# Index tiles first, logits between the matmul steps of later tiles, and a shorter keep in the threshold search

## The reference, cut to what matters

```
u = rmsnorm(h, norm_mix[0])
a_q, a_ckv, i_q, i_k, i_w, b_qkv, b_z, b_beta, b_a = split(u @ w_in)
# indexer, for each block of 128 query rows (4 heads of 64)
logits = einsum('bqhd,bsd->bqhs', q_idx, k_idx)
score  = einsum('bqh,bqhs->bqs', w, relu(logits))      # causal by chunks of 64
idx    = top_k(score, 256)                             # which latents a query sees
...
y_b = gated_deltanet(b_qkv, b_z, b_beta, b_a, ...)     # starts with silu(causal_conv(b_qkv))
```

## Time and profile before

| | |
|---|---|
| median of 3 timed runs | 2788.07 us (2785.03 to 2789.04) |
| the profiled execution | 2780.74 us, its span 2778.9 us |
| PE busy, share of the span | 94% |
| DVE busy | 60% |
| ACT, POOL busy | 35%, 10% |
| mean granted TensorE clock | 0.957 |

### The profile page before, as it was taken

How to read it: one execution, slowest core, us unless ns; L and a number is a source line. 1 busy time by engine, 2 the same in 40 slices (tenths; PEclk the granted TensorE clock), 3 DMA queues, 4 the chain that set the end, 5 groups by cost and what they waited for, 6 DMA issues and landing times.

```text
span 2778.9 us, 32118 instructions
## 1 busy us (share of the span) xinstructions
PE 2625.5 (94%) x12096; PEld 2086.8 (75%) x12096; DVE 1661.8 (60%) x2672; ACT 969.3 (35%) x1615; POOL 264.5 (10%) x268
## 2 busy tenths in 40 slices
PE   8998987888998899999999999898899999999998
PEld 7666666878755477888888878676687888888787
DVE  4179997677455357756664354763768665653444
ACT  4232221111154344333333233443744333332333
POOL 3004525444000000000001000000000000000000
PEclk7989998899699999999999999999999999999999
DMA  5211110000100043232235434111132322335443
GB/s 161 69 38 31 38 31 1 0 0 1 46 1 1 23 136 114 84 91 84 68 92 194 162 125 139 36 46 46 31 99 106 91 70 82 91 95 215 145 137 106
DMA packets 207166, 217.27 MB, mean 78 GB/s; under 512 B 12496, under 2 KB 174304, under 8 KB 203568
## 3 DMA queue, kind: packets, MB, share of 16 engines
q1 hardware_dynamic: 204080, 196.13, 22.6%
q0 software_dynamic: 2944, 19.24, 1.9%
HBM read 172.35 MB, written 42.47 MB: 77 GB/s over the span
## 4 chain that ended last, share of the span: by engine, by line
PE 79%; DVE 14%; issue 3%; ACT 2%; POOL 0%; DMA 0%; DVEq 0%; SPq 0%; POOLq 0%; ACTq 0%
PE ps L329 21%; PE ps L330 20%; PE ps L331 20%; DVE met L1948 4%; PE ps L2673 2%; DVE bT L1925 2%; PE ps L2155 1%; PE ps L2168 1%; PE ps L2650 1%; DVE thr L1978 1%; PE ps L2661 1%; PE ps L2164 1%; PE ps L1757 1%; PE ps L423 1%; PE ps L1056 1%
## 5 line engine op out<-in xcount | busy, mean ns | idle before, releaser
L318 DVE TENSOR_TENSOR wlo<-wraw,whi 128x1024 fp32r<-128x1024 f32 x152 | 186.7, 1230 | 389.9 <-ACT whi L312 389.6
L312 ACT ACTIVATE whi<-wraw 128x1024 fp32r<-128x1024 f32 x166 | 174.8, 1054 | 354.4 <-PE ps L331 341.3
L329 PE MATMUL ps<-ahi,whi 128*128 128x512 f32 x704 | 276.5, 393 | 6.2 <-DVE hT L956 3.8
L330 PE MATMUL ps<-alo,whi 128*128 128x512 f32 x704 | 275.1, 391 | 0.0
L331 PE MATMUL ps<-ahi,wlo 128*128 128x512 f32 x704 | 275.1, 391 | 0.0
L329 PE MATMUL ps<-uhi,whi 128*128 128x512 f32 x608 | 245.3, 403 | 19.8 <-DVE bT L1935 10.1
L329 PE MATMUL ps<-q_T,whi 128*128 128x512 f32 x640 | 249.2, 389 | 1.6 <-ACT upr L757 1.6
L331 PE MATMUL ps<-q_T,wlo 128*128 128x512 f32 x640 | 249.0, 389 | 0.0
L330 PE MATMUL ps<-q_T,whi 128*128 128x512 f32 x640 | 249.0, 389 | 0.0
L329 PE MATMUL ps<-q_B,whi 128*128 128x512 f32 x608 | 238.9, 393 | 2.4 <-DVE q_B L488 2.4
L330 PE MATMUL ps<-ulo,whi 128*128 128x512 f32 x608 | 239.7, 394 | 0.0
(11 more groups left out here) (464 smaller groups left out, 4894.5 us busy)
## 6 DMA issues: line engine op xcount, KB each, us to landing
wraw<-in_ffn_w_down_dram SPq DMA_DIRECT2D x88, 512.0 KB, 3.5
wraw<-in_ffn_w_gate_dram SPq DMA_DIRECT2D x44, 512.0 KB, 5.3
araw<-acts SPq DMA_DIRECT2D x88, 256.0 KB, 3.7
wraw<-in_ab_w_in_dram SPq DMA_DIRECT2D x24, 512.0 KB, 3.8
park<-hT POOLq DMA_DIRECT2D x3, 4096.0 KB, 11.4
wraw<-in_ffn_w_up_dram SPq DMA_DIRECT2D x24, 512.0 KB, 5.3
acts<-sgA SPq DMA_DIRECT2D x12, 1024.0 KB, 4.6
raw<-in_ffn_w_up_dram SPq DMA_DIRECT2D x20, 512.0 KB, 4.0
```

Source lines behind the costliest of these rows:

```text
L312: nc.scalar.activation(as_raw(whi[:, t.slot, :]), raw, ACT.Copy).then_inc(S("w_high"), 1)
L318: eng.tensor_tensor(as_raw(wlo[:, t.slot, :]), raw, as_raw(whi[:, t.slot, :]).bitcast(F32), ALU.subtract).then_inc(S("w_split"), 1)
L329: nc.tensor.matmul(dst, wh, xh, start=start, stop=False, **kw)
L330: nc.tensor.matmul(dst, wh, xl, start=False, stop=False, **kw)
```

## The change

1. The tiles come in the order index queries, index queries, index key, compressed KV. The doubling (`twice`) moves from tile 3 to tile 2, and the copy of the compressed KV to DRAM by POOL waits for the fourth move, not the first.
2. The small product follows tile 2. Its transposes follow the first 8 steps of tile 3.
3. The logits go in 12 pairs of heads (parities 0 and 1 alternate for each piece of 512), each followed by 2 steps of the tiles 3, 4 and 5. A pair waits until both relus of the pair before are done. The other steps of tiles 5 and 6 follow. ACT and DVE do units 0 to 7 in iteration 3 and 8 to 23 in iteration 4, where DVE also masks, computes the gates and calls `select_start`.
4. `bits_of` gives one step to each of tiles 5, 6 and 7, then 14 to tiles 8 to 19 (two at 11 and 19), then 1, 2, 1, 2: again 23.
5. `select_keep` with a bit known when the program is built shifts the flag to the bit's place and ors it in, one instruction in place of two, and raises `sel_ok` by an instruction of its own. The 8 steps of the delta rule's loop keep the old form.

```diff
-    order = [("ab", CKV0), ("ab", IQ0), ("ab", IQ0 + P), ("ik", IK0)]
+    order = [("ab", IQ0), ("ab", IQ0 + P), ("ik", IK0), ("ab", CKV0)]
     order += [("ab", AQ0 + P * j) for j in range(4)]
...
     for i in range(2):
-        w_load(sp_, Tile(n_ab + i), ab_v[:, :, (CKV0, IQ0)[i]:(CKV0, IQ0)[i] + P])
+        w_load(sp_, Tile(n_ab + i), ab_v[:, :, IQ0 + i * P:IQ0 + (i + 1) * P])
     for i in range(1, 5):
...
-n_ab = first.get(("ab", CKV0), 0)
+n_ab = first.get(("ab", IQ0), 0)
 rel = [acc, at("relB", [P, SEQ], 44 * KB)]
...
 SEL = NB - 2
+RELU_AT = {3: range(0, 8), 4: range(8, 24)}
 met = at("met", [P, 2, SEQ], 112 * KB, mybir.dt.bfloat16)
...
-    steps = [0] * 6 + [2, 2] + [1, 1, 1, 2, 1, 1, 1, 2, 1, 1, 1, 2] + [1] * 4
+    steps = [0] * 5 + [1, 1, 1] + [1, 1, 1, 2, 1, 1, 1, 1, 1, 1, 1, 2] + [1, 2, 1, 2]
     assert sum(steps) == EARLY
...
     pool.dma_start(park, hT[:, :, :]).then_inc(S("parked"), 16)
-    pool.wait_ge(S("pa_moved"), 1)
+    pool.wait_ge(S("pa_moved"), 4)
     pool.dma_start(aside[0], tmp[0][:, :]).then_inc(S("aside0"), 16)
...
              {(0, 0, 3): lambda: norm_spread(pe, 1, 7)})
-    for i in range(2, 5):
-        tile(i)
+    tile(2)
     pe.wait_ge(S("wsm_split"), 2)
...
     last.then_inc(S("small_done"), 1)
-    tile(5)
+    def tile_steps(a, b):
+        for s in range(a, b):
+            i, (h, k) = 3 + s // 16, divmod(s % 16, KT)
+            if s % 16 == 0:
+                pe.wait_ge(S("pa_moved"), i - 1)
+                w_ready(pe, t[i])
+            last = three_pass(pair(i % 2)[:, rows_of(h)], whi[:, t[i].slot, k * P:(k + 1) * P],
+                              wlo[:, t[i].slot, k * P:(k + 1) * P], uhi[:, k, rows_of(h)], ulo[:, k, rows_of(h)],
+                              k == 0, k == KT - 1)
+            if s % 16 == 15:
+                last.then_inc(S("w_used"), 1)
+    def logits(n):
+        b, h0 = UNITS[n]
+        pe.wait_ge(S("ix_relu"), n)
+        for w0 in range(0, WID[b], HALF):
+            w1 = min(w0 + HALF, WID[b])
+            for odd in range(2):
+                part = slice(64 * odd, 64 * odd + 64)
+                last = pe.matmul(pair(2 + odd)[:, w0:w1], iq[part, h0 // 2, b * P:(b + 1) * P], ik[part, w0:w1],
+                                 start=True, stop=True)
+                if w1 == WID[b]:
+                    last.then_inc(S("ix_logits"), 1)
+    tile_steps(0, 8)
     pe.wait_ge(S("small_copied"), 1)
...
     last.then_inc(S("small_turned"), 1)
-    for n, (b, h) in enumerate(UNITS):
-        if n == 0:
-            pe.wait_ge(S("small_moved"), 3)
-        if n >= 2:
-            pe.wait_ge(S("ix_relu"), n - 1)
-        part = slice(64 * (h % 2), 64 * (h % 2) + 64)
-        for w0 in range(0, WID[b], HALF):
-            w1 = min(w0 + HALF, WID[b])
-            last = pe.matmul(pair(2 + h % 2)[:, w0:w1], iq[part, h // 2, b * P:(b + 1) * P],
-                             ik[part, w0:w1], start=True, stop=True)
-        last.then_inc(S("ix_logits"), 1)
-    for i in range(6, 24):
+    tile_steps(8, 10)
+    pe.wait_ge(S("small_moved"), 3)
+    pe.wait_ge(S("pa_moved"), 3)
+    for p in range(len(UNITS) // 2):
+        logits(2 * p)
+        tile_steps(10 + 2 * p, 12 + 2 * p)
+    tile_steps(10 + len(UNITS), 64)
+    for i in range(7, 24):
         tile(i)
...
-    def relus():
-        for n, (b, h) in enumerate(UNITS):
+    def relus(i):
+        for n in RELU_AT.get(i, ()):
+            b, h = UNITS[n]
             act.wait_ge(S("ix_logits"), n + 1)
...
         if i + 2 < 24:
-            w_high(act, t[i + 2], twice=i + 2 == 3)
+            w_high(act, t[i + 2], twice=i + 2 == 2)
         if i == 15:
...
             unit_roots(act)
+        if i == 3:
+            small()
+        relus(i)
+        if i == 5:
+            act.wait_ge(S("gt_in"), 2)
+            softplus(act, None, None, aval[:, :, :].rearrange("p b h -> p (b h)"), sp, 32, 0)
         tile_done(act, t[i])
         if i < 8:
-            dst = {0: tmp[0][:, :], 1: iq[:, 0, :], 2: iq[:, 1, :], 3: ik[:, :]}.get(i)
+            dst = {0: iq[:, 0, :], 1: iq[:, 1, :], 2: ik[:, :], 3: tmp[0][:, :]}.get(i)
             if i >= 4:
...
             act.activation(dst, pair(i % 2), ACT.Copy).then_inc(S("pa_moved"), 1)
-            if i == 4:
+            if i == 2:
                 act.wait_ge(S("small_done"), 1)
                 act.activation(acc[0:12, :], pair(3)[0:12, :], ACT.Copy).then_inc(S("small_copied"), 1)
-            if i == 5:
-                small()
-                relus()
-                act.wait_ge(S("gt_in"), 2)
-                softplus(act, None, None, aval[:, :, :].rearrange("p b h -> p (b h)"), sp, 32, 0)
         elif i < 20:
...
-    def scores():
-        for n, (b, h) in enumerate(UNITS):
+    def scores(i):
+        for n in RELU_AT[i]:
+            b, h = UNITS[n]
+            if n == 0:
+                dve.wait_ge(S("small_moved"), 1)
             dve.wait_ge(S("ix_relu"), n + 1)
...
+    def hide():
         dve.wait_ge(S("ix_added"), len(UNITS))
...
         if i + 2 < POOL_LOW:
-            w_low(dve, t[i + 2], twice=i + 2 == 3)
-        if i == 5:
-            scores()
+            w_low(dve, t[i + 2], twice=i + 2 == 2)
+        if i in RELU_AT:
+            scores(i)
+        if i == 4:
+            hide()
             gates()
...
             decay_small(dve)
-        if i in (6, 7):
+        if i in (5, 6, 7):
             for k in bits_of(i):
...
     dve.wait_ge(S("sel_ok"), 2 * k + 1)
+    if isinstance(k, int):
+        dve.scalar_tensor_tensor(out=mag[:, :], in0=okm[:, :], scalar=30 - k, in1=mag[:, :],
+                                 op0=ALU.logical_shift_left, op1=ALU.bitwise_or).then_inc(S("sel_kept"), 1)
+        dve.sem_inc(S("sel_ok"), 1)
+        return
     dve.tensor_tensor(thr[:, :], okm[:, :], bit(k), ALU.mult).then_inc(S("sel_ok"), 1)
```

## The result

The changed kernel takes **2753.15 us** (median; 2750.14 to 2756.33), the kernel before, timed beside it, 2786.55 (2781.25 to 2789.04): a ratio of 0.9877, interval 0.9860 to 0.9893. The profiled execution took 2751.75, its span is 2749.9. Its first normalization ends 1.9 us later than in the profile of before (the first L458 stands at 32.84 against 30.92), which has to be kept in mind when times are compared. The line of the new shift-and-or is L2009.

The account below looks back on a forecast made before the run. PE was taken to set the pace until 172.1 us, DVE from 175.1 to 416.3. Convolution 23.4 us earlier, then 201.7 for 204.45, splits 0.8 less: 26.9 off the median 2788.1, 2761.2 us; 8-in-10 range 2755 to 2776.

Parts of the forecast that it names:

- PE up to the convolution: PE's tiles and logits before the convolution: it can start at 188.5 us against 211.9, a gain of 23.4.
- the wide pair: Logits pairs of 640 to 1024 columns, taken as bound by ACT: 2.98 to 4.26 us each.
- DVE ready by then: DVE before the convolution: its work ends at 179 us, leaving it idle for 9, so PE decides the start.
- DVE behind it: DVE from convolution to delta rule: 201.7 us against 204.45, from +6.0 search step, -4.8 waits, -4.0 shorter keep.
- the 0.8: The two splits at the delta rule's start, no longer held up by POOL's first product: 0.8 us less.
- Rival 1: Logits loop: halves do not overlap when parities alternate, giving 2775.3 us; chance 0.20 together with a partly low clock.
- rival 2: Logits loop: the clock falls for all of it, +27.2 us, cancelling the gain, 2788 us; chance 0.06.
- rival 3: Logits loop and following tiles: the clock stays low to tile 6's end, +47.6 us, 2809 us; chance 0.03.
- Rival 4: Search steps in the convolution: DVE's waits behind POOL vanish, up to 23 us, PE then binding, about 2748; chance 0.05.
- Rival 5: Search steps: the shorter keep gains 0 a step, giving 2765 us; counted within the main forecast's 0.63.
- The timed runs lie 7.3 above it: Last step of the sum: carries the profiled execution's 2753.8 us over to a timed median of 2761.2.

Follow-up runs that it names:

- fill_idle: The changed kernel with one search step moved from tile 19 to tile 7, into DVE's idle time before the convolution: 2752.02 us, ratio 0.9872 to the kernel before.
- one_block: The changed kernel with all 12 logits pairs in one block and the tile steps between them moved behind: 2780.19 us, ratio 0.9968 to the kernel before.
- dve_splits: The changed kernel with the low parts of the weights of tiles 10 to 23 made by DVE instead of POOL: 2746.41 us, ratio 0.9857 to the kernel before.

## Why the prediction was right, and where it failed

**PE up to the convolution: nearly right, 1.7 us too dear.** The first pair came at 108.36 with a start 1.9 late, so 106.4 for 106.7. The loop took 36.8 for 38.4. The term at fault is the wide pair: 4.26 at 1024 against 4.01 measured, 3.83 against 3.59 at 896, 3.40 against 3.16 at 768, and 2.98 against 2.87 at 640, in all 1.7. The pairs of 640 and 768 did not wait for ACT at all; priced as bound by PE, as the narrow ones were, they come to 2.83 and 3.04. The 0.2 for the switch to half the rows was added there to the 2.02 from start to relu; but the first relu of a pair starts 143.75 - 141.73 = 2.02 behind PE's first record, as without a switch. From the row after the loop the way back costs its 0.1 to 0.2, as booked; on the way in nothing shows. From start to first tap the two profiles differ by 25.1, the sum said 23.4.

**DVE ready by then: right.** With the 1.9 of the later start taken off, the mask comes at 145.6 for 147.6 and the first counts are done at 155.9 for 157.9, both early with the pairs. The terms themselves fit: from the next-to-last relu to the mask 3.81 for 3.8, from there to the end of the first counts 10.24 for 10.25, idle 9.86 for 9. `fill_idle` shows that this idle was worth a step of the search.

**DVE behind it: right.** From first tap to the splits 201.86 for 201.7, at 0.2 us a step for the keep, the two waits at the end gone and no others behind tile 12; the splits took 2.36, and the 0.8 came. From first tap to first diagonal product 204.7 against 208.2: 3.4 gained for 3.55.

**Rivals.** Rival 1 fell on the pairs' 1.99, rivals 2 and 3 on the clock of 1.00; `one_block` shows how near rival 2 was: without the steps between, the clock falls. Rival 4 fell in the changed kernel, and `dve_splits` shows what it takes. Rival 5 fell on the 0.19 a step.

**The step that failed** is the last of the sum: "Behind 420 nothing is changed, and the delta rule waits for DVE, so the shift goes through to the end". It put at nothing what lies outside the stage. In the means of the profiles that is 5.3 us: a delta rule 4.7 and a rest 1.2 shorter, less a start 0.6 longer. The instructions there are the same but for two steps of the search that have the short keep in the delta rule too, which I had overlooked (0.4 us at 0.19 each); what makes the rest of the 5.3 stays open.

The whole miss of 8.05 adds up as 5.3 from that step, 1.3 from the stage (28.2 in the means for 26.9), and 1.5 from the median of before, which was 2788.07 in the three runs of the forecast and 2786.55 beside the changed kernel. "The timed runs lie 7.3 above it" only carries the shift over to the median of before, and would have been sound if both kernels drew alike. But the profile it was read from was a short draw: against the mean of five it had a start 1.6, a delta rule 2.9 and a rest 1.7 shorter, and a stage 1.0 longer. The changed kernel's median lies only 1.4 above its profiled execution. That 2780.7 - 26.9 = 2753.8 comes within 0.7 of the measured 2753.15 is luck: a short draw of before stands in for what the changed kernel does in the mean. And the range's low end, 2755, left 6 us for scatter, for the terms and for rival 4 together, where the timed runs of before alone cover 2778 to 2795 over the sessions.

## What to carry to other kernels

A sum of the trace's terms gives the shift from one profiled execution; before it is set on a median, look how that execution stands in a stage whose clock comes and goes, and widen the range by that stage's scatter (here 9 us in a delta rule of 342 over nine profiles), on top of the terms' own errors. And take several profiles of both kernels before you say that nothing changed behind the edit. Put dense work between units that wait for another engine: here it filled the waits and kept the granted clock at 1.00 (0.50 without it). An instruction that is short by itself but waits behind POOL was not made cheaper by rewriting it with the same two operands in SBUF; take the POOL instruction away that it waits for, as long as DVE's added work is less than the wait (1.2 for 2.3 here).

## What the runs showed of the hardware

- A shift-and-or on 128 x 6 with both operands in SBUF took 2.32 us beside POOL's split and 0.17 without it, ending 0.03 behind the split.
- Matmuls of two parities in different halves of the array's rows, alternating piece by piece, streamed as one: 1.99 us for two units of 1024, with no visible cost for entering the half-row form, 24 changes of it in the loop included.
- With full-row steps between them the half-row logits kept a granted clock of 1.00; without the steps, behind 10 us with PE busy 4.6 of them, it went to 0.50. It was 1.00 again at 138 to 146 us, in the same block, and 0.63 over the last pair.
- The delta rule, unchanged but for the two short keeps, took from 337.9 to 348.5 us over the profiles of all kernels (348.5 in `one_block`), in sequences that repeat to 0.5 us from one kernel to another.
